# Feature projections: the high and the low part of the tokens in one moving operand, the third product added on VectorE

## The reference, cut to what matters

```
u = h @ w_in                      # first block: 1024 x 7964
proj = h @ w_in[l] + b_in[l]      # second block: 1024 x 1280
```

```
xbc = silu(causal_dwconv(sxbc, w, b))          # 768 features, 4 taps over the tokens
qk  = silu(causal_dwconv(mqk, w, b))           # 512 features
y = lax.conv_general_dilated(u, w[:, None, :], ..., padding=[(3, 0)], feature_group_count=ch)
```

## Time and profile before

| | us |
|---|---|
| median of 3 executions | 2541.64 |
| lowest and highest | 2538.16, 2542.71 |
| profiled execution, its own time | 2543.85 |
| span of its trace (first to last instruction) | 2541.7 |
| TensorE busy, weight loads busy | 2246.0 (88%), 1796.5 (71%) |
| VectorE, ScalarE, GpSimd busy | 1597.8 (63%), 1288.2 (51%), 515.7 (20%) |

### The profile page before, as it was taken

One profiled execution on the slowest core, in us unless ns is written; L12 is line 12 of the kernel. 1 busy time (PEld: TensorE's weight loads), 2 busy tenths in 40 slices (PEclk: granted clock), 3 DMA queues, 4 the chain that ended last, 5 costly groups with the idle time before them and its releaser, 6 DMA issues.

```text
span 2541.7 us, 26117 instructions
## 1 busy us (share of the span) xinstructions
PE 2246.0 (88%) x10762; PEld 1796.5 (71%) x10762; DVE 1597.8 (63%) x1539; ACT 1288.2 (51%) x1300; POOL 515.7 (20%) x183
## 2 busy tenths in 40 slices
PE   6789688999778969899999999999967799877997
PEld 5667455887667756587787887877836488666886
DVE  2654445554276554788888888888955445455544
ACT  5454335443544324576676766766743443333442
POOL 2468555001435625200000000000030500000000
PEclk9899789999889978999999999999988899988999
DMA  7345446655533524799999999999962566532551
GB/s 253 117 165 180 151 129 204 208 192 159 173 128 106 178 86 157 225 351 338 358 329 343 365 322 332 367 339 349 364 244 67 168 195 210 172 127 81 184 186 63
DMA packets 387788, 550.49 MB, mean 217 GB/s; under 512 B 21048, under 2 KB 295096, under 8 KB 386768
## 3 DMA queue, kind: packets, MB, share of 16 engines
q1 hardware_dynamic: 383600, 534.82, 63.4%
q10 hardware_dynamic: 4064, 13.95, 1.5%
HBM read 547.58 MB, written 1.15 MB: 216 GB/s over the span
## 4 chain that ended last, share of the span: by engine, by line
PE 77%; DVE 11%; ACT 5%; POOL 5%; issue 1%; DMA 1%; ACTq 0%; POOLq 0%; DVEq 0%
PE bank L406 74%; POOL wlo L896 3%; PE bank L427 2%; DVE wlo L896 2%; ACT whi L890 1%; DVE arena L1352 1%; POOL small L1933 1%; DVE xn L1410 1%; DVE arena L1493 1%; DVE arena L1491 0%; POOL small L1931 0%; DVE scoresB L1419 0%; DMA xn<-in_lmask 0%; DVE outputs_lo L1723 0%; DVE rowbuf L1453 0%
## 5 line engine op out<-in xcount | busy, mean ns | idle before, releaser
L890 ACT ACTIVATE whi<-raw 128x2048 fp32r<-128x2048 f32 (+1 forms) x509 | 971.3, 1910 | 503.3 <-PE bank L406 488.2
L896 DVE TENSOR_TENSOR wlo<-raw,whi 128x2048 fp32r<-128x2048 f32 (+1 forms) x413 | 950.5, 2306 | 386.3 <-ACT whi L890 386.1
L896 POOL TENSOR_TENSOR wlo<-raw,whi 128x2048 fp32r<-128x2048 f32 x96 | 452.0, 4720 | 1426.7 <-DVEq L921 828.0
L406 PE MATMUL bank<-whi,hThi 128*128 128x512 f32 (+2 forms) x1104 | 440.9, 399 | 19.9 <-DVE wlo L896 8.8
L406 PE MATMUL bank<-wlo,hThi 128*128 128x512 f32 (+2 forms) x1104 | 432.2, 391 | 0.0
L406 PE MATMUL bank<-whi,hTlo 128*128 128x512 f32 (+2 forms) x1104 | 431.0, 390 | 0.0
L406 PE MATMUL bank<-whi,slots_hi 128*128 128x512 f32 x704 | 282.7, 402 | 1.9 <-issue 1.9
L406 PE MATMUL bank<-wlo,slots_hi 128*128 128x512 f32 x704 | 277.8, 395 | 0.0
L406 PE MATMUL bank<-whi,slots_lo 128*128 128x512 f32 x704 | 277.5, 394 | 0.0
L406 PEld LDWEIGHTS bank<-whi,hThi 128*128 128x128 f32 x1104 | 214.8, 195 | 66.1 <-DVE wlo L896 9.6
L406 PEld LDWEIGHTS bank<-whi,hTlo 128*128 128x128 f32 x1104 | 213.8, 194 | 43.5
(11 more groups left out here) (296 smaller groups left out, 2841.2 us busy)
## 6 DMA issues: line engine op xcount, KB each, us to landing
raw<-in_moe_w SPq DMA_DIRECT2D x352, 512.0 KB, 5.7
raw<-in_moe_w SPq DMA_DIRECT2D x88, 1024.0 KB, 7.3
raw<-in_w_in SPq DMA_DIRECT2D x72, 1024.0 KB, 5.1
raw<-in_ada_w SPq DMA_DIRECT2D x48, 1024.0 KB, 5.1
raw<-in_ffn_w SPq DMA_DIRECT2D x44, 512.0 KB, 4.9
raw<-in_w_gate SPq DMA_DIRECT2D x44, 512.0 KB, 4.0
raw<-in_w_up SPq DMA_DIRECT2D x44, 512.0 KB, 5.0
raw<-in_w_down SPq DMA_DIRECT2D x22, 1024.0 KB, 4.9
```

What stands on the lines that cost most here:

```text
L406: m = mm(dst, l_, r_, start=start and i == 0, stop=stop and i == len(pairs) - 1)
L890: s.then_inc(s.unit.activation(slot_of_ring(whi, p, NSPLIT)[:, 0:n], slot_of_ring(raw, p, NRAW)[:, 0:n], ACT.Copy), ("hi", p), sem="weight ...
L896: e.then_inc(e.unit.tensor_tensor(slot_of_ring(wlo, p, NSPLIT)[:, 0:n], slot_of_ring(raw, p, NRAW)[:, 0:n], slot_of_ring(whi, p, NSPLIT)[: ...
```

## The change

`hThi` and `hTlo` become the two halves of one tile `hT`. In a feature projection one matmul now streams 512 columns, the 256 high parts of the tokens and after them the 256 low parts, past the high part of the weights; the bank's left half then holds high by high and its right half high by low. A second matmul of 256 columns adds low by high to the left half. So a projection fills a bank of its own, with a semaphore of its own, and the sum of the two halves is left to the reader: ScalarE copies the left half to SBUF (`high_products`), and VectorE adds the right half to it in place (`third_product`) and frees the bank.

```
-            def project_features(w, c, stage, bank, at):
+            def project_features(w, c, stage, bank):
+
                 for tt in range(NT):
                     t.wait_ge(("hT", stage, tt))
-                return product(bank[:, at:at + T], [((w[0][:, k, c:c + P], w[1][:, k, c:c + P]), (hi3[:, k, :], lo3[:, k, :]))
-                                                    for k in range(KD)])
+                for k in range(KD):
+                    mm(bank[:, :], w[0][:, k, c:c + P], both_parts[:, k], start=k == 0, stop=False)
+                    m = mm(bank[:, 0:T], w[1][:, k, c:c + P], hi3[:, k, :], start=False, stop=k == KD - 1)
+                return m
 
             def two_features(name, w, c0, stage, lo_on="V"):
                 read, parts = piece(name, full_piece(w, c0), lo_on)
-                bank = t.take(name)
                 for j in range(2):
-                    m = project_features(full(parts), j * P, stage, bank, j * T)
-                t.then_inc(m, ("full", name), read)
+                    bank = t.take((name, j))
+                    m = project_features(full(parts), j * P, stage, bank)
+                    t.then_inc(m, ("full", (name, j)), *([read] if j else []))
...
+            def high_products(dst, name):
+
+                s.wait_ge(("full", name))
+                s.then_inc(act(dst, s.bank(name)[:, 0:T], ACT.Copy), ("two", name))
+
             def conv_in(l, name, bank_name, pad3, conv3, i):
-                s.wait_ge(("full", bank_name), (name + "_padded", l))
-                s.then_inc(act(pad3[:, 2 * i:2 * i + 2, PAD:], tiles(s.bank(bank_name)[:, :]), ACT.Copy), ("free", bank_name))
-                s.own()
+                for j in range(2):
+                    high_products(pad3[:, 2 * i + j, PAD:], (bank_name, j))
                 for c in (2 * i, 2 * i + 1):
+                    s.wait_ge((name + "_padded", l), (name + "_in", l, c))
                     s.then_inc(act(conv3[:, c, :], pad3[:, c, 0:T], ACT.Identity, scale=col(name + "_w", l, c),
                                    bias=col(name + "_b", l, c)), (name + "_first", l, c))
...
+            def third_product(dst, name, *done, bias=None):
+                v.wait_ge(("two", name))
+                low = v.bank(name)[:, T:2 * T]
+                v.then_inc(tensor(dst, dst, low, ALU.add) if bias is None else stt(dst, low, bias, dst, ALU.add, ALU.add),
+                           ("free", name), *done)
+
-            def conv_in(l, name, pad3, conv3, i, n, done):
+            def conv_in(l, name, bank_name, pad3, conv3, i, n, done):
                 both = 2 * i, 2 * i + 1
+                for j, c in enumerate(both):
+                    third_product(pad3[:, c, PAD:], (bank_name, j), (name + "_in", l, c))
                 for k in range(1, CONV_K):
...
```

More of the change, by code:

```diff
@@ L525, in mixer_step @@
                     bank = t.take(("z", l))
-                    t.then_inc(project_features(full(parts, P), 0, here, bank, 0), ("full", ("z", l)), read)
+                    t.then_inc(project_features(full(parts, P), 0, here, bank), ("full", ("z", l)), read)
                 elif step == "alpha":
@@ L778, in second_mixer @@
                 bank = t.take(("k2", l))
-                t.then_inc(project_features(wf, 0, here, bank, 0), ("full", ("k2", l)))
+                t.then_inc(project_features(wf, 0, here, bank), ("full", ("k2", l)))
                 bank = t.take(("v2", l))
@@ L1054, in mixer_step @@
                 elif step in ("p0.0", "p0.1"):
[L1055 to L1058, removed]
+                    for j in range(2):
+                        high_products(tiles(rot_raw)[:, 2 * int(n) + j, :], (("p0", l, int(n)), j))
                 elif step == "p0.2":
@@ L1082, in mixer_step @@
                 elif step == "p3.0":
[L1083 to L1086, removed]
+                    s.wait_ge(("y", l, 1))
+                    high_products(glaq, (("p3", l), 0))
+                    high_products(glak, (("p3", l), 1))
                 elif step == "p3.1":
@@ L1090, in mixer_step @@
                         bank = s.bank((("p3v", l), tt))
-                        s.then_inc(act(tok3(gv)[:, tt], bank[:, 0:MIX], ACT.Copy), *([("gv", l)] if tt else []))
+                        s.then_inc(act(tok3(gv)[:, tt], bank[:, 0:MIX], ACT.Copy, scale=GLA_DK ** -0.5), *([("gv", l)] if tt else []))
                         side(("p3v", l), bank, gr, MIX, tt)
@@ L1192, in second_mixer @@
                 features((l, "mix2"))
+                for i in range(2):
+                    for j in range(2):
+                        high_products(qraw3[:, 2 * i + j, :], (("q2", l, i), j))
+                high_products(qraw3[:, 4, :], ("k2", l))
                 def attend(tt, n):
@@ L1425, in mixer_step @@
                 if step == "z":
-                    v.wait_ge(("free", ("z", l)))
+                    v.wait_ge(("z_copied", l))
+                    bank = v.bank(("z", l))
+                    v.then_inc(tensor(gate_feat[0:16, :], gate_feat[0:16, :], bank[32:48, T:2 * T], ALU.add), ("gate_feat", l))
+                    v.then_inc(tensor(row(DT), row(DT), bank[0:NH, T:2 * T], ALU.add))
+                    v.then_inc(tensor(row(CJ), row(CJ), bank[64:64 + NH, T:2 * T], ALU.add))
+                    v.then_inc(tensor(row(LF), row(LF), bank[96:96 + NH, T:2 * T], ALU.add), ("free", ("z", l)))
+                    v.own()
                     v.then_inc(scalar(row(DT), row(DT), col("dt_bias", l, rows=NH), None, ALU.add))
@@ L1463, in mixer_step @@
                     v.own()
+                elif step in ("p0.0", "p0.1"):
+                    i = int(n)
+                    for j in range(2):
+                        third_product(tiles(rot_raw)[:, 2 * i + j, :], (("p0", l, i), j), *([("rot_raw", l, i)] if j else []))
+                elif step == "p3.0":
+                    third_product(glaq, (("p3", l), 0))
+                    third_product(glak, (("p3", l), 1))
                 elif step == "p0.2":
@@ L1469, in mixer_step @@
                         v.then_inc(v.unit.memset(pad1_3[:, :, 0:PAD], 0.0), ("ssd_conv_padded", l))
-                    conv_in(l, "ssd_conv", pad1_3, tiles(conv1), int(n), NSX, ("conv1", l, int(n)))
+                    conv_in(l, "ssd_conv", ("p1", l, int(n)), pad1_3, tiles(conv1), int(n), NSX, ("conv1", l, int(n)))
                 elif step == "p1.3":
@@ L1477, in mixer_step @@
                         v.then_inc(v.unit.memset(mva4[:, :, :, HD:HD + 1], 1.0))
-                    conv_in(l, "ml_conv", pad2_3, tiles(conv2), int(n), NMQ, ("conv2", l, int(n)))
+                    conv_in(l, "ml_conv", ("p2", l, int(n)), pad2_3, tiles(conv2), int(n), NMQ, ("conv2", l, int(n)))
                 elif step == "p3.1":
@@ L1774, in second_mixer @@
                 for i in range(2):
-                    v.wait_ge(("full", ("q2", l, i)))
                     for j in range(2):
-                        v.then_inc(scalar(qraw3[:, 2 * i + j, :], v.bank(("q2", l, i))[:, j * T:(j + 1) * T], col("b_q", l, 2 * i + j), None, ALU.add),
-                                   *([("qraw", l, i), ("free", ("q2", l, i))] if j else []))
+                        third_product(qraw3[:, 2 * i + j, :], (("q2", l, i), j), *([("qraw", l, i)] if j else []), bias=col("b_q", l, 2 * i + j))
                 rotate(0)
-                v.wait_ge(("full", ("k2", l)))
-                v.then_inc(scalar(qraw3[:, 4, :], v.bank(("k2", l))[:, 0:T], col("b_k", l), None, ALU.add), ("kraw", l), ("free", ("k2", l)))
+                third_product(qraw3[:, 4, :], ("k2", l), ("kraw", l), bias=col("b_k", l))
                 v.wait_ge(("full", ("v2", l)))
```

10 lines of the change are left out of this document (6 added, 4 removed).

## The result

The changed kernel takes 2547.57 us (median of nine executions, 2545.29 to 2551.95), the kernel before 2541.64 us (2538.16 to 2542.71). The ratio is 1.0027, with a 95% interval of 1.0016 to 1.0037: 6.9 us more, between 4.1 and 9.4. The forecast was 2545.5 us, in a range of 2540 to 2550.5, slightly slower. So the time lies in the range and on the slow side, as forecast, and the sum of +3.9 us was some 3 us short. But 6.9 us is past the 0.2% (5.1 us) that the prediction called the least that can be told: there "slower" had a chance of 0.43 and "within" one of 0.51, so the less favoured of the two came. The profiled execution took 2548.9 us.

A forecast was written before the change was run, and what follows sets the result against it. TensorE was taken to bound most projections, but VectorE and ScalarE the p1 convolutions. 6.4 - 2.3 - 0.2 = +3.9 us on the profiled 2543.85 us, less 2.2 us to the median, gave 2545.5 us, range 2540 to 2550.5.

The forecast's parts named there:

- the sum: Whole kernel: 6.4 us paid in convolutions, less 2.3 on TensorE and 0.2 in second-layer p2.0, +3.9 us.
- TensorE's saving: Feature projections: 0.0131 us less per k-step, counting for 174 full-clock k-steps on the chain, 2.3 us.
- The six convolutions: p1.0, p1.1, p1.2 in two layers: VectorE's add and ScalarE's first tap delay VectorE's taps, 6.4 us slower.
- six by 1.07 = 6.4: p1.0 to p1.2, two layers: add 421 ns, first tap 596 ns, two hand-overs of some 0.03 us: 1.07 us each.
- The serial hand-over: Rival, six p1 convolutions: both adds and both first taps in a row, 2.03 us each, +9.7 us; chance 0.13.
- The adds hide: Rival, p1 convolutions: ScalarE's copies come early and VectorE finds room, -2.5 us, 2539.1 us; chance 0.13.
- Two strips as two matmuls: Rival, feature projections: the two-strip operand saves nothing on TensorE, +6.2 us, 2547.8 us; chance 0.07.
- What was costed at nothing: Adds and copies in z, p0, p3.0, q and k, p2.1 and first-layer p2.0 hidden, bank turns harmless: 0 us.
- TensorE's wait before "tokcol": After p1, sign in the profile after: the 7.6 us wait grows to near 12 us.
- The chances: Whole kernel's outcome: slower 0.43, within 0.2% 0.51, faster 0.06.

The follow-up runs named there:

- second pair: Traces of after_again (changed kernel) and before_again (kernel before), each run once more: spans 2542.8 and 2535.9 us, 6.9 us apart.
- after_again: The changed kernel run once more, unaltered, for a second trace and set of times: 2547.12 us, ratio to before 1.0028.
- before_again: The kernel before run once more, unaltered, for a second trace: 2538.94 us, ratio to before 0.9995.
- early_adds: Changed kernel with p1.1 and p1.2 banks copied a step earlier and added in VectorE's gaps; GpSimd's splits moved too: 2542.43 us, ratio to before 1.0012.
- conv_only: The kernel before with the change made for the convolution features (p1 and p2) alone: 2554.01 us, ratio to before 1.0052.
- conv_no_add: Changed kernel with the high-weights, low-tokens product computed but not added in the convolution features: 2539.89 us, ratio to before 0.9998.
- three_matmuls: Changed kernel with each bank filled by three passes of 256 columns per k instead of 512 plus 256: 2550.97 us, ratio to before 1.0035.
- p1_old: Changed kernel with the six p1 groups projected, evicted and tapped as before, p2 keeping the change: 2544.92 us, ratio to before 1.0013.

## Why the prediction was right, and what it missed

**TensorE's saving: right for each k-step and in place; its total is not shown.** k-steps of 0.347 and 0.640 us. Gains by the second pair of traces, the forecast's behind them: 0.37 us in "z" to "p0.2" of the first layer (0.41), 0.19 in the second (0.42), 0.3 in "p2.0" of the second (0.32 with its reader), 0.09 in each "p3.0" (0.21), 0.5 in the first q and k (0.47). All that lies outside the six steps and the one long stretch adds up to -2.3 us, against the sum's -2.3 and -0.2. That is so near partly by luck: 0.8 us of it are in the second q and k, where after_again has 3.8 us at the low clock and before_again 5.1. The same remainder, each trace held against before_again, runs from -2.3 to +6.5 us. Its mean is +1.9 in the six traces with the joint pass in q and k and +3.6 in the seven without (early_adds, whose splits moved, left out). That is 1.7 us less, with a scatter of 2 to 3 us from trace to trace. What the clock takes back in "p3.0" is in it.

**The six convolutions: right in mechanism, mis-sized.** The step that was short is "six by 1.07 = 6.4"; it measured 7.5. Four of the six cost 1.15 to 1.19 us: the hand-over itself takes 1.00 us (76.77 to 77.77), and the taps behind it start with 0.49 us to the next one where the other four take 0.42 each, and run 2.18 us where the earlier trace rows have 1.99. The taps of before began under the end of the split; after a wait they don't. "p1.0" costs 1.55 and 1.25 us. In the first layer both adds (0.67) and 0.07 us of issue stand before ScalarE's tap, whose wait should end with the first add. By the trace's records of ScalarE's sequencer the wait is over at 65.66 us, 0.05 after the first add, and the tap still starts at 66.02. conv_only has it the other way about, 1.25 us in the first layer and 1.52 in the second. Why ScalarE starts late isn't settled.

**The serial hand-over** (2.03 us each, a rival) is excluded by the same rows, but for that part in "p1.0".

**The adds hide** is excluded by conv_no_add: leaving them out gives 7.7 us by the medians, and 7.5 in its six p1 steps.

**Two strips as two matmuls** is excluded by the k-step, and three_matmuls agrees.

**What was costed at nothing** held for the work itself. "p2.1": two adds stand at 151.20 us, and the taps behind them at 152.29:

```profile
151.20 0.75 DVE L1359 TENSOR_TENSOR arena<-arena,bank 128x256 f32<-128x256 f32 x2 [2.14 <-ACT arena L1008]
152.29 3.96 DVE L1371 SCALAR_TENSOR_TENSOR arena<-arena,cols 128x256 f32<-128x256 f32 x2 [0.34 <-ACT arena L1018]
```

The first tap takes 3.57 of these 3.96 us and ends 0.3 us behind GpSimd's split (150.97 us, 4.61 long), as in the earlier trace rows. The shift of the second pair stays within 0.05 us from 91 to 215 us. No wait for a bank appeared, in any layer.

**Not in the sum at all:** the 1.75 us of the attention stretch. The sum took the clock as it stood in the trace of before, for each matmul at a time. With 7.5 - 2.3 + 1.75 = 6.9 us the account gives the second pair's difference, as it must, and the two ratios (6.9 and 7.1 us) agree. The mean of the traces leads there by other terms, as an estimate: 7.5, less 1.7, and 1.2 for the attention stretch, which is 1.8 us over its short form in the six traces and 0.55 in the seven. That TensorE's earlier end of q and k is what moves the low stretch there is argued from seven traces against seven, not shown. So is that the joint pass draws such a stretch onto "p3.0", which rests on five cases of fourteen against none of fourteen. What else moves such stretches stays open, and with it why conv_only and p1_old stand 7 and 6 us over their sums. The long attention stretch is 1.9 and 1.7 us of that, and p1_old's two long "p3.0" are 2.8.

**TensorE's wait before "tokcol": wrong**, 9.4 us instead of near 12. The two later splits delay the weights of "p1.3" as well, so its wait for them grew from 3.6 to 5.5 us, and only what was left of the delay fell on "tokcol". The sum of both waits grew by 3.7 us (4.8 in the second pair).

**The chances** contain a slip: the parts named for "faster" (0.05, and what 0.13 for the hidden adds leaves beside the 0.10 put within) come to 0.08, not 0.06.

**The Trainium skill's** fixed cost for a warm matmul of about 2.5 ns ("TensorE: Matmul & The Clock Gate", section "Wait — 56ns, not 53.3ns?") would have made the saving 0.9 us for all 352 k-steps, an estimate. The trace disagrees: a matmul less saved 13 ns in each k-step at full clock, and 0.45 us over the 40 k-steps of the first q and k, where 2.5 ns each give 0.1.

## What to carry to other kernels

Cost a reader's change by the order of hand-overs behind the operation that ends last: each pair of adds, 0.34 us of it on the chain, brought 1.2 us with it, because a second engine had to answer it, and the engine that was relieved was waiting anyway. Work with a free operand belongs in a gap ahead of that point, not behind it. And for differences of some us, take two traces of each kernel before reading one difference: the first pair here gave 4.8 us, the second 6.9, and both hold the same 7.5 us for the edited steps. Compare the edited places by themselves, and only the rest by the total.

## What the runs showed of the hardware

- While GpSimd splits, VectorE's taps and row operations with all operands in SBUF are held to its end, and the adds with one operand in PSUM are not. Above, two adds from a bank take 0.75 us inside such a split, and the two taps behind them 3.96. In the trace of the changed kernel twelve of the new adds lie wholly inside a split of GpSimd, and each takes 0.41 to 0.42 us. Not every operation in SBUF is held: a reciprocal of 128x2 elements takes 0.17 us inside a split (at 1026.18 us). In "z", two small operations with a scalar on 4 x 256 elements take 4.72 us each beside two splits (35.01 to 44.44 us). The four adds behind them (1.41 us) start when the splits are over, so this place says nothing of adds:

```profile
35.22 4.72 DVE L1453 TENSOR_SCALAR rowbuf<-rowbuf,cols 4x256 f32<-4x256 f32 x1
39.87 4.72 DVE L1454 TENSOR_SCALAR rowbuf<-rowbuf,cols 4x256 f32<-4x256 f32 x1
44.62 1.41 DVE L1359 TENSOR_TENSOR arena<-arena,bank 128x256 f32<-128x256 f32 x4
```

The Trainium skill ("SBUF — State Buffer", section "SBUF: two separate sides") says that VectorE with two inputs in SBUF, or in a two-port mode, and GpSimd exclude each other for a whole instruction; the trace agrees. That it spares the adds of this change is shown by the twelve.

- Among "p1.2"'s scans the same blocking sits on the chain: 4.59 us for an operation of 0.42. No run here removed it and kept TensorE fed; that is what a next version of this kernel could try.
- One stretch of TensorE at the low clock more or less cost 1.3 us for the same 26 matmuls, 1.4 to 1.5 in "p3.0" and 1.6 to 2.0 in a stretch of 114 us with the same 408 matmuls, which took 114.0 to 114.1 or 115.7 to 116.1 us and nothing between. The two traces of before lie 5.8 us (0.23%) apart, by such stretches and the DMA wait named above.
- The granted clock of the profile says 1.00 from 27 to 32 us in the trace of before, while 256 columns take the 0.2137 us of 1.2 GHz there. In the first burst the spacing tells the level, not the clock's record.
